# Head pairs in the windowed attention, a mask that holds the counts, and the attention half of the output projection first

## The reference, cut to what matters

```python
def hybrid_mixer(h, w_in, conv_w, g_attn_out, g_conv_out, w_out):
    proj = h @ w_in
    q, k, v, bg, cg, xc = jnp.split(proj, 6, axis=-1)
    ...
    for window, dilation in DILATED_PATTERNS:      # (128, 1), (512, 4), (2048, 16)
        o, lse = dilated_window_attention(q, k, v, window, dilation)
    ...
    mix_w = jax.nn.softmax(jnp.stack(lses, axis=0), axis=0)
    attn = jnp.einsum('pbsh,pbshe->bshe', mix_w, jnp.stack(outs, axis=0).astype(jnp.float32))
    ...
    conv = short_gated_conv(bg, cg, xc, conv_w)    # bg * causal_conv3(cg * xc)
    merged = jnp.concatenate([rms_norm(attn, g_attn_out), rms_norm(conv, g_conv_out)], axis=-1)
    return merged @ w_out
```

## Time and profile before

| | |
|---|---|
| median of 3 runs | 2351.41 us (2347.61 to 2352.49) |
| the profiled execution | 2345.92 us, of which the span is 2344.0 us |
| PE busy | 1997.5 us, 85% of the span |
| DVE busy | 1580.3 us, 67% |
| ACT busy | 1017.0 us, 43% |
| POOL busy | 614.7 us, 26% |

### The profile page before, as it was taken

One profiled execution on the slowest core, in us unless ns is written; L12 is line 12 of the kernel. 1 busy time (PEld: TensorE's weight loads), 2 busy tenths in 40 slices (PEclk: granted clock), 3 DMA queues, 4 the chain that ended last, 5 costly groups with the idle time before them and its releaser, 6 DMA issues.

```text
span 2344.0 us, 23866 instructions
## 1 busy us (share of the span) xinstructions
PE 1997.5 (85%) x8004; PEld 1246.4 (53%) x8004; DVE 1580.3 (67%) x2973; ACT 1017.0 (43%) x2122; POOL 614.7 (26%) x562
## 2 busy tenths in 40 slices
PE   3998889887777778799888988888888878989998
PEld 2975665322222223379866543433433326878987
DVE  7875766776667666578776777667677654665654
ACT  2342444444444444435334454444455444344543
POOL 0000034444444444200002444443444440400000
PEclk9999999999999999999998999999999999889999
DMA  7785579999999999786556999999999994333553
GB/s 288 287 307 203 216 293 421 420 421 422 421 422 421 421 421 419 303 329 226 211 218 272 421 422 421 420 421 421 419 412 422 421 421 164 108 117 126 181 182 141
DMA packets 112635, 761.93 MB, mean 325 GB/s; under 512 B 12881, under 2 KB 13665, under 8 KB 26369
## 3 DMA queue, kind: packets, MB, share of 16 engines
q0 software_dynamic: 76720, 549.67, 56.6%
q1 hardware_dynamic: 34832, 207.73, 23.9%
q10 hardware_dynamic: 960, 3.01, 0.4%
HBM read 759.32 MB, written 1.05 MB: 324 GB/s over the span
## 4 chain that ended last, share of the span: by engine, by line
PE 28%; DMA 14%; ACT 4%; DVE 4%; issue 2%; POOL 1%; DVEq 0%; SPq 0%; ACTq 0%; PEldq 0%; POOLq 0%
DMA uv<-in_peer_uv,p_idx 13%; PE pair L662 9%; PE pair L893 8%; PE pair L614 7%; PE pair L916 1%; ACT ring_high L1877 1%; PE pair L923 1%; DMA ring<-in_sgu_w_in 1%; DVE ring_low L1140 1%; DMA ada<-in_ada_w 1%; POOL uv L516 1%; ACT p_diag L2069 1%; PE pair L814 1%; ACT L2063 0%; DVE uv L1474 0%
## 5 line engine op out<-in xcount | busy, mean ns | idle before, releaser
L893 PE MATMUL pair<-uv,p_diag 128*128 128x512 f32 x1536 | 760.3, 630 | 192.4 <-ACT p_diag L2069 190.7
L1474 DVE CUSTOM_DVE_ANT_0 uv<-uv,p_h 128x1024 f32<-128x1024 f32 x384 | 470.4, 1225 | 340.9 <-DMA uv<-in_peer_uv,p_idx 339.6
L516 POOL DMA_INDIRECT uv<-in_peer_uv,p_idx x384 | 435.9, 1135 | 750.7 <-PE pair L893 588.6
L893 PEld LDWEIGHTS pair<-uv,p_diag 128*128 128x128 f32 x1536 | 279.9, 196 | 651.1 <-ACT p_diag L2069 385.2
L1140 DVE TENSOR_TENSOR ring_low<-ring,ring_high 128x2048 fp32r<-128x2048 f32 x148 | 336.3, 2288 | 127.1 <-ACT ring_high L1877 122.6
L2063 ACT ACTIVATE p_act<-p_dot 128x1 f32<-128x1 f32 x512 | 103.5, 202 | 653.5 <-DVE p_dot L1474 651.3
L1877 ACT ACTIVATE ring_high<-ring 128x2048 fp32r<-128x2048 f32 x148 | 278.5, 1907 | 167.9 <-DMA ring<-in_ret_w_in 42.4
L662 PE MATMUL pair<-hT_high,ring_high 128*128 128x256 f32 x992 | 286.7, 289 | 0.7 <-DVE hT_low L1150 0.6
L662 PE MATMUL pair<-hT_low,ring_high 128*128 128x256 f32 x992 | 281.4, 284 | 0.0
L662 PE MATMUL pair<-hT_high,ring_low 128*128 128x256 f32 x992 | 281.4, 284 | 0.0
L893 PE MATMUL pair<-uv_high,p_diag 128*128 128x512 f32 x512 | 245.6, 611 | 38.7 <-ACT p_diag L2069 38.6
(11 more groups left out here) (353 smaller groups left out, 2368.4 us busy)
## 6 DMA issues: line engine op xcount, KB each, us to landing
ada<-in_ada_w SPq DMA_DIRECT2D x50, 512.0 KB, 5.6
ring<-in_ret_w_in SPq DMA_DIRECT2D x24, 1024.0 KB, 5.0
ring<-in_sgu_w_in SPq DMA_DIRECT2D x24, 1024.0 KB, 7.5
ring<-in_peer_w_query SPq DMA_DIRECT2D x16, 1024.0 KB, 4.8
ring<-in_w_up SPq DMA_DIRECT2D x16, 1024.0 KB, 4.8
ring<-in_w_down SPq DMA_DIRECT2D x16, 1024.0 KB, 4.7
mod<-in_ada_w SPq DMA_DIRECT2D x30, 512.0 KB, 5.9
ring<-in_sgu_w_out SPq DMA_DIRECT2D x12, 1024.0 KB, 5.5
```

What stands on the lines that cost most here:

```text
L516: nc.gpsimd.indirect_dma_start(uv_rows[SLOT[l][s]].rearrange("p a d -> p (a d)"), None, experts, bass.IndirectOffsetOnAxis(ap=p_idx[:, k:k ...
L893: mm = nc.tensor.matmul(acc[:, half, :], p_diag[:, n % DIAGS, :], v[:, half * 512:(half + 1) * 512], start=(k == 0), stop=(k == PICKS - 1))
L1474: V.tensor_tensor_reduce(out=u, in0=u, in1=p_h[:, s // PICKS, :], scale=1.0, scalar=0.0, op0=ALU.mult, op1=ALU.add, accum_out=p_dot[:, n % ...
```

## The change

1. Attention runs in four **pairs of heads**. One mask addition, one maximum and one reciprocal serve two heads and both token tiles where they can; the PSUM slot of a pair holds four score tiles. Each pair's transposes still go head by head into the `small` buffers.
2. The **counts are put in the mask** as 8 log(many), so the exponential gives them. The multiplication by `b_many` goes, with its load; ScalarE sums the rows beside the exponential (`accum_out`), in four instructions for a pair, and PE waits for ScalarE alone.
3. The **rounds of attention stand among the blocks** of chunks 4, 5 and 3 (`chunk(c, kb)` is one block of a chunk). The last product with v stands inside the last block of chunk 3. The conversions `lows` and `highs` are placed block by block among them.
4. The **blocks of w_out are loaded and used with the attention half of both chunks first**. The sum of the convolution's squares stands between these two blocks, and `mcv_ready` is waited for after them. The turns of the first half of x stand before the last tile of the last block.
5. ScalarE squares the attention rows, in place of VectorE, and copies chunk 3 (`b_bgT`) after their root.

```diff
-    order = list(range(kt // BK))
-    return order[::-1] if mat == ("w_out",) else order
+    return list(range(kt // BK))
...
-    out += [("w_in", 2), ("w_in", 0), ("w_in", 1), ("att", 0), ("w_in", 4), ("att", 1), ("w_in", 5), ("att", 2), ("w_in", 3)]
-    out += [("att", h) for h in range(3, HEADS)]
...
-    out += turned(5) + [("attT", 0)]
-    for h in range(HEADS):
-        out += [("atto", h)] + ([("attT", h + 1)] if h + 1 < HEADS else []) + ([("conv_sq",)] if h == CONV_AT else [])
-    out += [("att_rows", t) for t in range(TT)] + turned(7)
+    def heads_turned(b):
+        return [("attT", 2 * b), ("attT", 2 * b + 1)]
+    out += turned(5) + heads_turned(0) + [("atto", 0)] + heads_turned(1) + heads_turned(2) + [("atto", 1), ("atto", 2)] + heads_turned(3) + [("atto", 3)]
+    out += [("att_rows", t) for t in range(TT)] + [("conv_sq",)] + turned(7)
...
+        places = [(n, kb) for n in ns for kb in k_order(name, kt)]
+        for n, kb in sorted(places, key=lambda place: place[1]) if inner > 1 else places:
+            blocks.append(ap[n, kb].rearrange("p (k n) -> p k n", k=BK))
...
                         pool.dma_start(b_mask, w["att_mask"]).then_inc(hyb_in, 16)
-                        pool.dma_start(b_many, w["att_many"]).then_inc(hyb_in, 16)
...
+                def att_turn(b):
+                    pe.wait_ge(e_ready, 4 * (b + 1))
+                    for j in range(2):
+                        softmax_turned("att", 2 * b + j, [b_e[:, b % 2, j, q * P:(q + 1) * P] for q in range(3)])
...
                 att_scores(0)
-                columns_product(("w_in", 4), ("w_in",), 4, hT)
+                chunk(4, 0)
                 att_scores(1)
+                chunk(4, 1)
                 att_turn(0)
-                columns_product(("w_in", 5), ("w_in",), 5, hT)
+                att_scores(2)
+                chunk(5, 0)
                 pe.wait_ge(*taken_sum(("w_in", 2)))
-                for h in range(HEADS):
-                    att_out(h)
-                    if h + 2 < HEADS:
-                        att_scores(h + 2)
-                    if h + 1 < HEADS:
-                        att_turn(h + 1)
-                    if h == 0:
-                        columns_product(("w_in", 3), ("w_in",), 3, hT)
-                    if h == CONV_AT:
+                att_out(0)
+                att_turn(1)
+                att_scores(3)
+                chunk(5, 1)
+                att_turn(2)
+                att_out(1)
+                chunk(3, 0)
+                att_out(2)
+                att_turn(3)
+                chunk(3, 1, lambda nt: att_out(3) if nt == 1 else None)
...
+                for c in range(2):
+                    open_sum(("w_out", c))
+                    for t in range(TT):
+                        mm = out_tile(c, 0, t)
+                    mm.then_inc(w_used, 1)
+                    if c == 0:
                         pe.wait_ge(sq_ready, 1)
...
+                pe.wait_ge(mcv_ready, 2)
+                for c in range(2):
                     for t in range(TT):
-                        pe.wait_ge(arow_ready, t + 1)
-                        name = ("att_rows", t)
-                        open_small(name)
-                        for q in range(4):
-                            mm = nc.tensor.transpose(small_of(name)[:, q * P:(q + 1) * P], b_att[:, t, q * P:(q + 1) * P], ident[:])
-                        mm.then_inc(small_ready, 1)
-                    for t in range(TT):
-                        pe.wait_ge(*taken_small(("att_rows", t)))
-
-                rows_product(("w_out", 0), ("w_out",), 0, b_mT, KD, halves)
-                def first_half(kb):
-                    if kb == 0:
-                        for t in range(TT):
-                            turn_group(7, b_h, t, 0)
-
-                rows_product(("w_out", 1), ("w_out",), 1, b_mT, KD, first_half)
+                        if c == 1 and t == 1:
+                            for tile in range(TT):
+                                turn_group(7, b_h, tile, 0)
+                        mm = out_tile(c, 1, t)
+                    mm.then_inc(sum_ready, 1)
...
+                    name, stat = ("att", b), b_stat[:, b % 2]
+                    for t in range(TT):
+                        part, keys = slice(t * P, t * P + (t + 1) * P), (t + 1) * P
+                        did(V.tensor_tensor(b_e[:, b % 2, :, part], sum_of(name)[:, :, t * S:t * S + keys],
+                                            bc(b_mask[:, part].unsqueeze(1), [P, 2, keys]), ALU.add), *(taken_sum(name) if t else (dve_step, None)))
+                    settle()
+                    for t in range(TT):
+                        did(V.tensor_reduce(stat[:, 0, 2 * t:2 * t + 2], b_e[:, b % 2, :, t * P:t * P + (t + 1) * P], AX_X, ALU.max))
+                    settle()
+                    did(V.tensor_scalar(stat[:, 1, :], stat[:, 0, :], -(HD ** -0.5), None, ALU.mult), smax_ready, b + 1)
...
+                    dve.wait_ge(e_ready, 4 * (b + 1))
+                    did(V.reciprocal(stat[:, 3, :], stat[:, 2, :]))
...
                 att_max(0)
+                lows(block_after(("w_in",), 4) - 1)
+                att_max(1)
+                lows(block_after(("w_in",), 4))
                 att_sum(0)
-                lows(block_after(("w_in",), 4))
-                att_max(1)
+                att_max(2)
+                lows(block_after(("w_in",), 5) - 1)
+                att_sum(1)
+                att_take(0)
+                att_max(3)
                 lows(block_after(("w_in",), 5))
-                att_step(0)
...
+                att_sum(2)
+                att_take(1)
+                lows(out_first)
+                att_sum(3)
+                att_take(2)
+                att_take(3)
+                dve.sem_inc(att_ready, 1)
+                lows(out_first + 1)
+                dve.wait_ge(att_sq, 1)
+                did(V.tensor_scalar(ms[:], hs[:, 0:2], 1.0 / 512, EPS, ALU.mult, ALU.add))
...
+                lows(out_first + 2)
+                name = ("conv_sq",)
+                dve.wait_ge(small_ready, SMALL[name] + 1)
...
+                lows(out_first + 5)
                 product_by_halves(7, ("w_out", 0), 0, x_gain)
-                lows(block_after(("w_out",), 1))
...
+                    stat = b_stat[:, b % 2]
+                    for t in range(TT):
+                        for j in range(2):
+                            i = 2 * t + j
+                            did(A.activation(b_e[:, b % 2, j, t * P:t * P + (t + 1) * P], b_e[:, b % 2, j, t * P:t * P + (t + 1) * P], ACT.Exp,
+                                             bias=stat[:, 1, i:i + 1], scale=HD ** -0.5, accum_out=stat[:, 2, i:i + 1]), e_ready, 4 * b + i + 1)
...
+                exponentials(0)
+                highs(block_after(("w_in",), 4) - 1)
+                exponentials(1)
+                highs(block_after(("w_in",), 4))
+                take_sum(("w_in", 4), columns(b_cgT))
+                take_turned(0)
+                exponentials(2)
+                highs(block_after(("w_in",), 5) - 1)
+                take_turned(1)
+                exponentials(3)
+                highs(block_after(("w_in",), 5))
+                take_turned(2)
+                highs(out_first)
+                take_turned(3)
+                highs(out_first + 1)
+                act.wait_ge(att_ready, 1)
+                for t in range(TT):
+                    did(A.activation(junk[:, t * 512:(t + 1) * 512], b_att[:, t, :], ACT.Square, accum_out=hs[:, t:t + 1]))
+                settle()
+                act.sem_inc(att_sq, 1)
+                act.wait_ge(cms_ready, 1)
...
+                take_sum(("w_in", 3), columns(b_bgT))
...
+                highs(out_first + 2)
+                act.wait_ge(cms_ready, 2)
+                did(A.activation(b_rs, b_rs, ACT.Sqrt), croot_ready, 2)
+                act.wait_ge(mcv_ready, 1)
+                high_of(b_mT[0][:, 4:8, :], b_cvn)
+                highs(out_first + 5)
...
-    mask = np.where(many > 0, 0.0, NEG).astype(f)
+    mask = np.where(many > 0, np.log(np.maximum(many, 1)) * HD ** 0.5, NEG).astype(f)
```

200 lines of the change are left out of this document (83 added, 117 removed).

## The result

The changed kernel took 2335.78 us (median of 6, 2332.95 to 2342.53), the kernel before 2350.16 us (median of 6, 2346.09 to 2353.11) on the same chip. The ratio is 0.9944, 95% interval 0.9933 to 0.9955: 13 us faster. The forecast was 3.5 us and a range whose lower end of 2340 lies above the measured time. The direction was right, the size was not.

The account below looks back on a forecast made before the run. Loss was PE's idle in the loop of heads 2 to 7 behind chunk 3 and the attention rows. w_out ending at 2088.0 against 2091.0 gives 3.0, the counts' load 0.5: 2351.41 - 3.5 = 2347.9 us, range 2340 to 2354.

Parts of the forecast that it names:

- Part 1, GpSimd's start: Attention rounds among the blocks: four rounds of about 8.7 us let GpSimd's convolution start at 2031.3, against 2018.9 before.
- Part 2, GpSimd's length: GpSimd's convolution: 21.0 us of its own plus up to 8.3 held by VectorE; squares ready at 2060.5.
- Rival B's second case: Conversions hold GpSimd little, squares come 6.6 us earlier: 2340.2 us; chance 0.22 together with B's first case.
- Part 3: Attention tail: attention block of w_out chunk 0 ends near 2053 or 2055, then PE idles 5 to 7 us.
- Part 4, conv_sq: Squares' sum on PE takes 3.0 us, between 1.8 and 3.6, done at 2063.5.
- Part 4, the end: Last blocks of w_out: 11.4 + 0.9 + 2.4 us after 2070.4, plus 2.9 for half clock, ending at 2088.0.
- Part 5: Small parts: dropping the counts' load of 192 KB gives 0.5 us, the count instructions no further gain.
- D: Rival: PE waits inside chunk 3's last block for copies of pair 3's transposes; time and chance within those of A.
- B's first case: Rival: clock stays full over short idles, end at 2082.7, 2342.6 us; chance 0.22 together with the second case.
- A: The forecast itself with errors on rounds, GpSimd's hold and clock: 2344 to 2352 us; chance 0.62.
- C: Rival: half clock from the wait before `conv_sq` to w_out's end, 2360.0 us; chance of any loss 0.16.
- three marks that were to show the forecast wrong: GpSimd's convolution under 25 us, its start before 2026, or the clock at 1.00 from 2045 to 2088.

Follow-up runs that it names:

- fill_gap: Changed kernel plus four matmuls that nobody reads, run in PE's wait inside chunk 5; 2331.53 us, ratio 0.9932 to the kernel before.
- pool_longer: Changed kernel with GpSimd doing the convolution's first tap multiplications twice; 2341.73 us, ratio 0.9972 to the kernel before.
- take_early: Changed kernel with VectorE scaling pair 0's output before it converts block 0 of chunk 3; 2333.39 us, ratio 0.9939 to the kernel before.
- third_low_later: Changed kernel with the conversion of w_out's third block moved behind the convolution's scaling; 2334.92 us, ratio 0.9946 to the kernel before.

## Why the prediction was wrong, point by point

The forecast put the stage's end at 2088.0, which is +99.0; it came at +89.1. The step that failed is PE's idle before `conv_sq`: 5 to 7 us with half clock behind it were forecast, and it was 1.76 us at full clock. It rests on a start and a length of GpSimd's work that were both taken too late and too long. The missing 9.9 us are in four terms of the sum, all on the chain that the prediction had named:

- **Part 1, GpSimd's start**: forecast 2031.3, +42.3; measured +39.6. 2.7 us. A round took 8.31 instead of 8.75, four times (1.8), above all because the conversion followed the first exponential after 1.77 (1995.94 to 1997.71) instead of 2.1. A pair's scores, twice in the sum at 1.7, took 0.93 at full clock: the first round began at +1.05 instead of +1.7 (0.65), and pair 3's came 3.5 us behind the conversion before it instead of 4.0 (0.5). Hand-offs and `b_uT` took 0.3 more. The 1 us for half clock was right (fill_gap), and so was the idle of some 3.5 us in chunk 5 (3.16).
- **Part 2, GpSimd's length**: forecast 29.2, measured 26.3. 2.9 us. Its own time was 26.3 less three holds of 1.9 to 2.0, 20.5, as against 21.0 (0.5). The holds were 5.8 and not 8.3 (2.4). The hold was mis-sized: I charged each conversion with its whole 2.3 us although the row behind it gave 3.8 for two, that is 1.9 each, and the scaling of the attention rows with 1.4, where it held GpSimd not at all but was itself lengthened, 1.84 instead of 1.4. That it can be VectorE that waits is also seen in pool_longer, where the scaling took 3.51, and in take_early, where a conversion took 3.94. The direction was right: conversions hold GpSimd. Rival B's second case, that they hold it little, is refuted by third_low_later.
- **Part 3**: the squares came at +65.8 and not at +71.5. PE was done with the attention block at +64.1, close to the forecast's +64.0 (2053 at full clock). So the idle of 5 to 7 us became 1.76, at a granted clock of 1.00 around it. This is the step on which the rest turned.
- **Part 4, conv_sq**: 3.0 was taken, at half clock; it took 1.99, at full. 1.0 us. The root chain of 6.9 us was right (2060.41 to 2067.35 is 6.94).
- **Part 4, the end**: from the first conv block, 11.4 + 0.9 + 2.4 + 2.9 = 17.6 were forecast, and 14.2 passed. 3.4 us. The 2.9 for half clock did not come, since the wait of 2.4 us before the turns came as two of 0.66 and 0.74; PE's own work was 0.5 more.

2.7 + 2.9 + 1.0 + 3.4 = 10.0. Of these, 3.9 are half clock that didn't come, and the terms hang together: because GpSimd was 5.6 us earlier, PE's wait was 1.76 us, and no half clock stood behind it. pool_longer, which gives back 3.7 us of it, gets a wait of 2.73 us and 1.7 us of half clock's cost at once. I had added errors on the slow side: each round, each hold and each share of the clock was taken at its upper bound or near it, and the clock shares were priced as if they didn't depend on the others. With every one of them at its lower end the range would have reached below 2340. Small slips of the prediction's sums change nothing: GpSimd's length is 29.3 in one place and 29.2 in the next, the root chain of before is 6.8 by its rows and not 6.9, and rival B's first end is 2082.9 by the shares of the clock that were added.

**Part 5**: the mask's half microsecond can't be seen. The start of the stage varies by far more between runs, and 12.9 of stage leave next to nothing of 13 to explain. **D** did not come about: PE waits 0.34 us at most in chunk 3.

The **rivals**: B's first case (full clock, end at +93.7) had the clock nearly right, but with it the long rounds and holds of A. C, half clock to the end, did not come. The profile had one piece of evidence against it that was put too low: in the kernel before, too, PE came back to full clock once it worked densely, as from 2073.1 on the earlier trace rows. Of the three marks that were to show the forecast wrong, one came true: the clock row at 1.00 from 2045 to 2088. GpSimd started at 2032 and not before 2026, and took 26.3 us and not under 25.

**The hold.** The row spoke, and speaks, for a hold of 1.9 to 2.0 us by a conversion with two SBUF inputs. The prediction weighed against it the Mode Summary alone. The Trainium skill has the rule that fits elsewhere ("SBUF — State Buffer", SBUF: two separate sides): of a VectorE operation in a two-port mode or with two SBUF inputs and a GpSimd operation that reads SBUF, the one that starts first keeps the shared port pair to its end, and the other waits. By that rule, the addition that starts 0.17 us behind the conversion waits for its end, and the trace agrees: 4.39 instead of 2.41 us. It agrees the other way round as well: the conversion of take_early, which began 0.62 us into GpSimd's addition, took 3.94 instead of 2.29 us. One case doesn't fit it: a conversion that began during a single tap was not lengthened (last section).
